# The end of an expert loop on Trainium2: one step moved, placement matrices built in pieces, one more tile summed by TensorE

## The chip, the core and the metric

The kernel runs on one core of one Trainium2 chip. The metric is the device time of a launch in microseconds; the median of three runs is used. A core has TensorE (PE, with its weight loads shown apart as PEld), VectorE (DVE), ScalarE (ACT), GpSimd (POOL) and SyncE (SP), which here issues most of the DMAs. Each engine works through its own queue in order and waits on semaphores.

## The reference

One transformer block over 512 rows of 1024: attention (left out here), a layer norm, a mixture of 32 experts in four groups of which each row uses two, and a second layer norm.

```python
SEQ, D_MODEL, N_GROUPS, EXPERTS_PER_GROUP, TOP_K, D_EXPERT = 512, 1024, 4, 8, 2, 256

def hierarchical_moe(x, w_group, b_group, w_expert, b_expert, w_gate, w_up, w_down):
    g_logits = (x @ w_group).astype(jnp.float32) + b_group
    g_prob = jax.nn.softmax(g_logits, axis=-1)
    g_gate, g_idx = lax.top_k(g_prob, 1)
    ...
    e_gate, e_idx = lax.top_k(e_prob, TOP_K)
    e_gate = e_gate / jnp.sum(e_gate, axis=-1, keepdims=True)
    combine = jnp.sum(jax.nn.one_hot(e_idx, EXPERTS_PER_GROUP, dtype=jnp.float32)
                      * e_gate[..., None], axis=2) * g_gate
    group_mask = jax.nn.one_hot(g_idx[..., 0], N_GROUPS, dtype=jnp.float32)
    y = jnp.zeros_like(x)
    for g in range(N_GROUPS):
        cw = (combine * group_mask[..., g:g + 1]).astype(x.dtype)
        hid = jax.nn.silu(jnp.einsum('bsd,edf->bsef', x, w_gate[g])) * jnp.einsum('bsd,edf->bsef', x, w_up[g])
        y = y + jnp.einsum('bsef,efd->bsd', hid * cw[..., None], w_down[g])
    return y

def reference(x, ...):
    for l in range(DEPTH):                                   # DEPTH is 1
        mix = hybrid_mixer(x, w_in[l], w_out[l], rel_bias[l])
        x = layer_norm(DEEPNORM_ALPHA * x + mix, ln1_g[l], ln1_b[l])
        ffn = hierarchical_moe(x, w_group[l], b_group[l], w_expert[l], b_expert[l],
                               w_gate[l], w_up[l], w_down[l])
        x = layer_norm(DEEPNORM_ALPHA * x + ffn, ln2_g[l], ln2_b[l])
    return x
```

## The kernel before

The 512 rows are T = 4 tiles of 128 (`hx`). After attention and the first layer norm, every row has a first and a second choice among the E = 32 experts; each expert has SLOTS = 64 places for rows. The part that the change touches is the loop over the experts and the stage behind it.

**The expert loop.** Experts go in pairs m; `get(m)` on GpSimd gathers a pair's rows into `xe`, TensorE turns them (`turn_x`). For an expert e TensorE does `gate_up(e)` (16 steps of 64 x 256 with `gate_w` and `up_w`), `turn_hidden(e)` (two transposes of the hidden rows) and `down(e)` (four products with `down_w`). Between them ScalarE does `silu(e)` and VectorE `product(e)` (the hidden rows) and `turned_out(e)` (the copy to `hidT`). Both engines copy one half each of down's result to `y_rows` (`first_half_out`, `second_half_out`), and GpSimd's `put(e)` scatters these to the DRAM table `expert_rows`, which has a row for each of the first and each of the second choices. Experts 30 and 31, the LAST pair, are not put: TensorE brings their rows to their places later. The order is written out by hand on each engine; TensorE's is: `gate_up(e+1)`, `turn_x` on odd e, the four transposes of `place` at e = 28 (L1590, behind a wait on all PLACED = 8 steps that build the matrices), `down(e)`, `turn_hidden(e+1)`.

**The weights.** Three matrices of 1 MB for each expert come over SyncE's queue into a ring of RING = 7 slots. `gate_w` and `up_w` of e are issued when `gate_up(e-7)` is done, `down_w` of e-1 behind them when its down is done. So the last ones are issued in the order gate/up 30, down 29, gate/up 31, down 30, down 31.

**The placement matrices.** `last_places` (L1133 to L1152) builds on VectorE: `again` (which row has which slot), then for both experts of the last pair `last_gate`, `gated` and `place`, and then diagonal matrices: `gate_diag` for the gates of each tile's second choices, `first_diag` for the first choices of tile BY_PE = 2. It stands behind expert 28's `turned_out` and uses the memory of ring slot 4, behind a wait on down 25.

**The last stage.** SyncE loads `first_y` and `second_y`, 512 KB for each tile, behind `put(28)` and `put(29)`. For each tile t TensorE adds in PSUM the rows of the last pair (`last_rows`, `place_T` by `y_rows`), for tile 2 the first-choice rows (`first_diag` by `first_y`) and the second-choice rows (`gate_diag` by `second_y`). VectorE does for the other tiles `add_first(t)` (L1230: `hx` plus gate by `first_y`), then for all `add_rest(t)` (L1239: plus the sum in PSUM, with the row sums for the mean; L1244: times `gain2`), and `finished(t)` (L1251) behind ScalarE's squares and root. SyncE stores each finished tile.

## Time and profile before

| | us |
|---|---|
| median of 3 runs (lowest, highest) | 566.36 (565.53, 567.29) |
| the profiled execution | 564.78 |
| its span | 563.1 |
| TensorE busy | 494.3 (88%) |
| VectorE busy | 250.3 (44%) |
| ScalarE busy | 184.1 (33%) |

The span is the time from the first to the last instruction of the profiled execution. The page puts 36% of the chain of work that ended last on TensorE, 9% on DMAs and 6% on VectorE. The share of busy time is an average over stages: in the expert loop the DMA engines are at 9 tenths or more of busy time in nearly every slice, in the last stage they are not. The rows further down are from the last 110 us.

### The profile page before, as it was taken

The page shows a single profiled execution, that of the slowest core. Times are in us where ns is not written, and L with a number is a line of the kernel's source. Part 1 is how long each engine was busy: PE and PEld are TensorE (multiplying, and loading weights), DVE is VectorE, ACT ScalarE, POOL GpSimd, SP SyncE. Part 2 cuts the span into 40 slices and gives each one's busy share as a digit, 9 for nine tenths or more (in the row PEclk, how much of TensorE's full clock was granted, in tenths as well). Part 3 has the DMA queues.
Part 4 walks back from the last instruction along what each step waited for, and adds up shares of the span by engine and source line. Part 5 has one row for each costly group of instructions (what it writes and reads, how often), then busy time and mean ns, then how long its engine had stood idle before and what let it go on. Part 6 is the DMA issues. An engine that isn't in the chain of part 4 may idle for free.

```text
span 563.1 us, 8062 instructions
## 1 busy us (share of the span) xinstructions
PE 494.3 (88%) x3068; PEld 326.1 (58%) x3068; DVE 250.3 (44%) x472; ACT 184.1 (33%) x377; POOL 149.3 (27%) x129
## 2 busy tenths in 40 slices
PE   4999999999999999799843899999998887878891
PEld 4788766766676766588632555555554454444440
DVE  3300256876766565600765533332332222215267
ACT  4212254465454555321513222322222222212222
POOL 3444435455413133133001222222222111210100
PEclk9999999999999999999975999999999998989997
DMA  6523221861211225199498799999999999999673
GB/s 242 169 76 113 75 75 39 319 105 38 76 38 38 76 75 208 56 348 420 167 415 307 321 370 416 414 415 415 414 415 418 415 416 418 415 416 417 245 273 149
DMA packets 53239, 144.12 MB, mean 256 GB/s; under 512 B 11014, under 2 KB 27414, under 8 KB 45008
## 3 DMA queue, kind: packets, MB, share of 16 engines
q1 hardware_dynamic: 48160, 134.40, 61.7%
q0 software_dynamic: 5040, 9.18, 4.4%
q8 instruction: 26, 0.43, 0.3%
q14 instruction: 13, 0.11, 0.1%
HBM read 135.45 MB, written 16.27 MB: 269 GB/s over the span
## 4 chain that ended last, share of the span: by engine, by line
PE 36%; DMA 9%; DVE 6%; issue 4%; SPq 2%; ACT 0%; POOLq 0%
PE bank L1498 16%; PE bank L1525 8%; DMA gate_w<-in_w_gate 5%; PE bank L1485 3%; DMA xe<-h_rows,idx_all 2%; PE bank L1278 2%; PE bank L1279 2%; PE bank L1280 2%; DMA second_y<-expert_rows 1%; SPq L379 1%; PE bank L1511 1%; DMA expert_rows<-y_rows,idx_odd 1%; PE bank L1500 1%; DVE hx L1239 1%; DVE hx L943 1%
## 5 line engine op out<-in xcount | busy, mean ns | idle before, releaser
L1498 PE MATMUL bank<-gate_w,xeT 128*64 128x256 f32 x512 | 122.7, 395 | 20.6 <-issue 18.9
L1500 PE MATMUL bank<-up_w,xeT 128*64 128x256 f32 x512 | 123.0, 396 | 0.0
L1498 PEld LDWEIGHTS bank<-gate_w,xeT 128*64 128x64 f32 x512 | 70.2, 142 | 54.4 <-issue 24.9
L513 POOL TENSOR_TENSOR w_lo<-raw,w_hi 128x1024 fp32r<-128x1024 f32 x28 | 71.2, 2543 | 89.2 <-ACT w_hi L629 89.2
L1500 PEld LDWEIGHTS bank<-up_w,xeT 128*64 128x64 f32 x512 | 70.2, 142 | 0.0
L1096 DVE TENSOR_TENSOR silu_hid<-silu_hid,bank 64x256 f32<-64x256 f32 x32 | 13.5, 423 | 117.8 <-ACT silu_hid L767 117.8
L1525 PE MATMUL bank<-down_w,hidT 128*64 128x512 f32 x256 | 61.3, 599 | 0.9 <-issue 0.9
L767 ACT ACTIVATE silu_hid<-bank 64x256 f32<-64x256 f32 x32 | 12.1, 377 | 129.9 <-PE bank L1500 129.9
L1278 PE MATMUL bank<-xT_hi,w_hi 128*128 128x512 f32 x128 | 53.6, 419 | 0.8 <-ACT values L648 0.8
L1280 PE MATMUL bank<-xT_lo,w_hi 128*128 128x512 f32 x128 | 50.7, 396 | 0.0
L1279 PE MATMUL bank<-xT_hi,w_lo 128*128 128x512 f32 x128 | 50.6, 395 | 0.0
L629 ACT ACTIVATE w_hi<-raw 128x1024 fp32r<-128x1024 f32 x28 | 29.6, 1057 | 42.9 <-PE bank L1280 27.2
L552 POOL DMA_INDIRECT xe<-h_rows,idx_all x16 | 17.2, 1076 | 79.5 <-PE bank L1485 68.4
L854 DVE TENSOR_TENSOR_SCAN fail<-fail 128x512 f32<-128x512 f32 (+3 forms) x32 | 27.0, 884 | 24.1 <-POOL fail L523 23.8
L669 ACT ACTIVATE wT<-bank 128x512 f32<-128x512 f32 (+3 forms) x64 | 24.3, 430 | 31.2 <-PE bank L1339 31.0
L1278 PEld LDWEIGHTS bank<-xT_hi,w_hi 128*128 128x128 f32 x128 | 24.1, 188 | 18.0 <-issue 11.4
L562 POOL DMA_INDIRECT expert_rows<-y_rows,idx_all x15 | 14.0, 934 | 73.5 <-DVE y_rows L1112 73.5
L1112 DVE COPY y_rows<-bank 64x512 f32<-64x512 f32 x32 | 22.2, 694 | 24.7 <-PE bank L1525 24.1
L1525 PEld LDWEIGHTS bank<-down_w,hidT 128*64 128x64 f32 x256 | 17.4, 136 | 22.9 <-issue 19.2
L758 ACT ACTIVATE xeT<-bank,shift_T,gain_T 128x128 f32<-128x128 f32 x64 | 24.1, 458 | 17.6 <-PE bank L1485 17.6
L775 ACT ACTIVATE y_rows<-bank 64x512 f32<-64x512 f32 x32 | 18.9, 591 | 30.7 <-PE bank L1525 30.3
L690 ACT ACTIVATE Z<-Z,nnear 128x512 f32<-128x512 f32 (+3 forms) x32 | 17.7, 555 | 34.2 <-DVE nnear L876 34.2
(183 smaller groups left out, 813.0 us busy)
## 6 DMA issues: line engine op xcount, KB each, us to landing
gate_w<-in_w_gate SPq DMA_DIRECT2D x32, 1024.0 KB, 24.8
up_w<-in_w_up SPq DMA_DIRECT2D x32, 1024.0 KB, 24.9
down_w<-in_w_down SPq DMA_DIRECT2D x32, 1024.0 KB, 24.4
raw<-in_w_in SPq DMA_DIRECT2D x24, 512.0 KB, 3.8
expert_rows<-xe SPq DMA_DIRECT2D x1, 4096.0 KB, 15.0
raw<-in_w_out SPq DMA_DIRECT2D x8, 512.0 KB, 4.3
hx<-in_x SPq DMA_DIRECT2D x4, 512.0 KB, 4.9
h_rows<-hx SPq DMA_DIRECT2D x4, 512.0 KB, 13.7
```

Of the source, the lines that this page charges most:

```text
L513: nc.gpsimd.tensor_tensor(lo[:, :], raw[:, slot, :], hi[:, :].bitcast(F32), ALU.subtract).then_inc(s_lo, 1)
L629: nc.scalar.activation(hi[:, :], raw[:, slot, :], ACT.Copy).then_inc(s_hi, 1)
L669: ins = nc.scalar.activation(wT[:, u % 2, h, 0:W[b]], TR[h][:, 0:W[b]], ACT.Copy)
L758: ins = nc.scalar.activation(xeT[:, m % 2, c, :], XE[:, c, :], ACT.Identity, bias=shift_T[:, c:c + 1], scale=gain_T[:, c:c + 1])
L854: ins = nc.vector.tensor_tensor_scan(f, f, f, 1.0, ALU.mult, ALU.min)
L1112: nc.vector.tensor_copy(y_rows[half(h), D // 2:], DN[h][1]).then_inc(s_yd, 1)
L1278: nc.tensor.matmul(dst, a_hi, b_hi, start=start, stop=False)
L1279: nc.tensor.matmul(dst, a_lo, b_hi, start=False, stop=False)
L1280: return nc.tensor.matmul(dst, a_hi, b_lo, start=False, stop=stop)
L1498: nc.tensor.matmul(GATE[h], xeT[:, m % 2, c, half(h)], gate_w[r][:, c, :], start=(c == 0), stop=(c == KD - 1))
L1500: mm = nc.tensor.matmul(UP[h], xeT[:, m % 2, c, half(h)], up_w[r][:, c, :], start=(c == 0), stop=(c == KD - 1))
L1525: mm = nc.tensor.matmul(DN[q][j], hidT[:, q, b, :], down_w[r][:, b, j * 512:(j + 1) * 512], start=(b == 0), stop=(b == FB - 1))
```

## The change

On TensorE, ScalarE and VectorE the loop gets a case of its own for e = 29 (E - 3): down 29 stands first, and gate/up 30 and 31 follow behind it, then the turn of expert 30's hidden rows; at e = 30 no gate/up is left. `last_places` is split: `slot_ranks` and expert 30's part stand behind `turned_out(26)`, expert 31's part behind `turned_out(27)`, the diagonals where the whole had stood, behind `turned_out(28)`. The wait of the first piece is on gate/up 25 rather than on down 25. BY_PE is now the tiles 2 and 3, so `first_diag` has two matrices, and VectorE's `add_first` for tile 3 is gone. On VectorE `add_rest(0)` stands ahead of `add_first(1)`.

```diff
...
         assert top[0] <= nc.sbuf_usable_end, (top[0], nc.sbuf_usable_end)
+        BY_PE = (T - 2, T - 1)
         spare = arena + 4 * SLOT
         again = at("again", [P, 2 * T, SLOTS], F32, spare)
         gated = at("gated", [P, 2 * T, SLOTS], F32, spare + 2048)
         place = at("place", [P, T, 2, SLOTS], F32, spare + 4096)
         place_T = at("place_T", [P, T, P], F32, spare + 6144)
         gate_diag = at("gate_diag", [P, T, P], F32, spare + 8192)
-        first_diag = at("first_diag", [P, P], F32, spare + 11264)
+        first_diag = at("first_diag", [P, len(BY_PE), P], F32, spare + 11264)
         last_gate = at("last_gate", [P, 2, 2, T], F32, spare + 10240)
         first_y = at("first_y", [P, T, D], F32, spare + SLOT)
         second_y = at("second_y", [P, T, D], F32, spare + SLOT + T * D * 4)
...
         PLACED = 8
         EARLY_AT = [(PAIRS - 2, 1), (PAIRS - 2, 3), (PAIRS - 1, 0), (PAIRS - 1, 1)]
-        BY_PE = T - 2
         def half(h):
...
             turned_half(1)
             first_half_out(0)
             for e in range(1, E):
-                if e + 1 < E:
+                if e == E - 3:
+                    first_half_out(e)
+                    silu(e + 1)
+                    silu(e + 2)
+                    continue
+                if e + 1 < E and e != E - 2:
                     silu(e + 1)
                 if e == E - 1:
                     nc.scalar.preload_act_table_set("sqrt_and_others")
...
                 ins.then_inc(s_place, 1)
                 dve.wait_ge(s_place, placed[0])
-            def last_places():
-                dve.wait_ge(s_dn, E - 6)
+            def slot_ranks():
+                dve.wait_ge(s_gu, E - 6)
                 then_place(nc.vector.tensor_tensor(
                     again[:, :, :], iota_f[:, :].unsqueeze(1).broadcast_to([P, 2 * T, SLOTS]),
                     rank[:, :, :].rearrange("p k t -> p (k t)").unsqueeze(2).broadcast_to([P, 2 * T, SLOTS]),
                     ALU.is_equal))
-                for h in range(2):
-                    then_place(nc.vector.tensor_tensor(last_gate[:, h, :, :], chosen[:, :, :, 2 * LAST + h],
-                                                       gate[:, :, :], ALU.mult))
-                    then_place(nc.vector.tensor_tensor(
-                        gated[:, :, :], again[:, :, :],
-                        last_gate[:, h, :, :].rearrange("p k t -> p (k t)").unsqueeze(2
-                                                                          ).broadcast_to([P, 2 * T, SLOTS]),
-                        ALU.mult))
-                    then_place(nc.vector.tensor_tensor(place[:, :, h, :], gated[:, 0:T, :], gated[:, T:, :], ALU.add))
+            def last_places(h):
+                then_place(nc.vector.tensor_tensor(last_gate[:, h, :, :], chosen[:, :, :, 2 * LAST + h],
+                                                   gate[:, :, :], ALU.mult))
+                then_place(nc.vector.tensor_tensor(
+                    gated[:, :, :], again[:, :, :],
+                    last_gate[:, h, :, :].rearrange("p k t -> p (k t)").unsqueeze(2).broadcast_to([P, 2 * T, SLOTS]),
+                    ALU.mult))
+                then_place(nc.vector.tensor_tensor(place[:, :, h, :], gated[:, 0:T, :], gated[:, T:, :], ALU.add))
+            def gate_diagonals():
                 for t in range(T):
                     ins = nc.vector.tensor_scalar(gate_diag[:, t, :], ident[:, :], gate[:, 1, t:t + 1], None, ALU.mult)
-                ins = nc.vector.tensor_scalar(first_diag[:, :], ident[:, :], gate[:, 0, BY_PE:BY_PE + 1], None, ALU.mult)
+                for j, t in enumerate(BY_PE):
+                    ins = nc.vector.tensor_scalar(first_diag[:, j, :], ident[:, :], gate[:, 0, t:t + 1], None, ALU.mult)
                 then_place(ins)
             n_passes = dve.value_load(passes_i[0:1, 0:1], min_val=1, max_val=S // SLOTS)
...
             turned_out(1)
             scaled_rows(3)
             for e in range(1, E):
-                if e + 1 < E:
+                if e == E - 3:
+                    second_half_out(e)
+                    product(e + 1)
+                    turned_out(e + 1)
+                    product(e + 2)
+                    continue
+                if e + 1 < E and e != E - 2:
                     product(e + 1)
                 if e % 2 == 1 and (e + 3) // 2 < MOE_PAIRS:
                     turned_tokens((e + 3) // 2)
                 second_half_out(e)
                 if e + 1 < E:
                     turned_out(e + 1)
+                if e == E - 7:
+                    slot_ranks()
+                    last_places(0)
+                if e == E - 6:
+                    last_places(1)
                 if e == E - 5:
-                    last_places()
+                    gate_diagonals()
                 if e == E - 4:
                     dve.wait_ge(s_turned, 1)
                     nc.vector.tensor_copy(place_T[:, :, :].rearrange("p t n -> p (t n)"), bank[:, 6, :]
...
             def add_rest(t):
                 n = T + t
-                if t != BY_PE:
-                    dve.wait_ge(s_res1, t + 1 if t < BY_PE else t)
+                if t not in BY_PE:
+                    dve.wait_ge(s_res1, t + 1)
                 dve.wait_ge(s_last, t + 1)
                 b = 2 * (T - 1 - t)
                 nc.vector.scalar_tensor_tensor(out=hx[:, t, :], in0=bank[:, b:b + 2, :].rearrange("p b n -> p (b n)"),
...
                                                in1=shift2[:, :], op0=ALU.mult, op1=ALU.add).then_inc(s_h, 1)
             add_first(0)
+            add_rest(0)
             add_first(1)
-            add_rest(0)
             add_rest(1)
             finished(0)
-            add_first(T - 1)
             for t in range(2, T):
                 add_rest(t)
                 finished(t - 1)
...
             down(0)
             turn_hidden(1)
             for e in range(1, E):
-                if e + 1 < E:
+                if e == E - 3:
+                    down(e)
+                    gate_up(e + 1)
+                    gate_up(e + 2)
+                    turn_hidden(e + 1)
+                    continue
+                if e + 1 < E and e != E - 2:
                     gate_up(e + 1)
                 if e % 2 == 1 and (e + 3) // 2 < MOE_PAIRS:
                     turn_x((e + 3) // 2)
...
                 b = 2 * (T - 1 - t)
                 pe.wait_ge(s_first[t], 32)
-                if t == BY_PE:
+                if t in BY_PE:
                     for j in range(2):
-                        nc.tensor.matmul(bank[:, b + j, :], first_diag[:, :], first_y[:, t, j * 512:(j + 1) * 512],
+                        nc.tensor.matmul(bank[:, b + j, :], first_diag[:, BY_PE.index(t), :], first_y[:, t, j * 512:(j + 1) * 512],
                                          start=False, stop=False)
                 for j in range(2):
                     mm = nc.tensor.matmul(bank[:, b + j, :], gate_diag[:, t, :], second_y[:, t, j * 512:(j + 1) * 512],
```

On TensorE, from the transposes of `place` to the end of the experts; `down_w0`, `1`, `2`, `3` are the ring slots of experts 28, 29, 30, 31, and `gate_w2`, `gate_w3` those of 30 and 31. Before:

```order
L1590 MATMUL bank<-ident_53,place_166 128x128 x4
L1525 MATMUL bank<-down_w0_106,hidT_163 64x512 x4
L1511 MATMUL bank<-ident_53,silu_hid_162 128x64 x2
L1498 MATMUL bank<-gate_w2_110,xeT_156 64x256
...
L1525 MATMUL bank<-down_w1_109,hidT_163 64x512 x4
L1511 MATMUL bank<-ident_53,silu_hid_162 128x64 x2
L1498 MATMUL bank<-gate_w3_113,xeT_156 64x256
...
L1525 MATMUL bank<-down_w2_112,hidT_163 64x512 x4
```

Now:

```order
L1616 MATMUL bank<-ident_53,place_166 128x128 x4
L1545 MATMUL bank<-down_w0_106,hidT_163 64x512 x4
L1531 MATMUL bank<-ident_53,silu_hid_162 128x64 x2
L1545 MATMUL bank<-down_w1_109,hidT_163 64x512 x4
L1518 MATMUL bank<-gate_w2_110,xeT_156 64x256
...
L1518 MATMUL bank<-gate_w3_113,xeT_156 64x256
...
L1531 MATMUL bank<-ident_53,silu_hid_162 128x64 x2
L1545 MATMUL bank<-down_w2_112,hidT_163 64x512 x4
```

Down 29 has moved ahead of gate/up 30, and the turn of expert 30's hidden rows from ahead of gate/up 31 to behind it.

On VectorE, the steps behind expert 28's `hidT`. Before:

```order
L1104 COPY hidT<-bank 128x128
L1136 TENSOR_TENSOR again<-iota_f,rank 128x512
L1141 TENSOR_TENSOR last_gate<-chosen,gate 128x8
L1143 TENSOR_TENSOR gated<-again,last_gate 128x512
L1148 TENSOR_TENSOR place<-gated 128x4x64
L1141 TENSOR_TENSOR last_gate<-chosen,gate 128x8
L1143 TENSOR_TENSOR gated<-again,last_gate 128x512
L1148 TENSOR_TENSOR place<-gated 128x4x64
L1150 TENSOR_SCALAR gate_diag<-ident,gate 128x128 x4
L1151 TENSOR_SCALAR first_diag<-ident,gate 128x128
L1096 TENSOR_TENSOR silu_hid<-silu_hid,bank 64x256
```

Now:

```order
L1109 COPY hidT<-bank 128x128
L1159 TENSOR_SCALAR gate_diag<-ident,gate 128x128 x4
L1161 TENSOR_SCALAR first_diag<-ident,gate 128x128 x2
L1101 TENSOR_TENSOR silu_hid<-silu_hid,bank 64x256
L1117 COPY y_rows<-bank 64x512
```

Seven steps have moved up to experts 26 and 27, and one diagonal is new.

On VectorE, the start of the last stage. Before:

```order
L1230 SCALAR_TENSOR_TENSOR hx<-first_y,gate,hx 128x1024 x2
L1239 SCALAR_TENSOR_TENSOR hx,row_sum<-bank,hx 128x1024
L916 TENSOR_SCALAR nmean<-row_sum 128x1
L1244 SCALAR_TENSOR_TENSOR first_y<-hx,nmean,gain2 128x1024
L1239 SCALAR_TENSOR_TENSOR hx,row_sum<-bank,hx 128x1024
L916 TENSOR_SCALAR nmean<-row_sum 128x1
L1244 SCALAR_TENSOR_TENSOR first_y<-hx,nmean,gain2 128x1024
L921 RECIPROCAL rstd<-std 128x1
L1251 SCALAR_TENSOR_TENSOR hx<-first_y,rstd,shift2 128x1024
L1230 SCALAR_TENSOR_TENSOR hx<-first_y,gate,hx 128x1024
```

Now:

```order
L1251 SCALAR_TENSOR_TENSOR hx<-first_y,gate,hx 128x1024
L1260 SCALAR_TENSOR_TENSOR hx,row_sum<-bank,hx 128x1024
L921 TENSOR_SCALAR nmean<-row_sum 128x1
L1265 SCALAR_TENSOR_TENSOR first_y<-hx,nmean,gain2 128x1024
L1251 SCALAR_TENSOR_TENSOR hx<-first_y,gate,hx 128x1024
L1260 SCALAR_TENSOR_TENSOR hx,row_sum<-bank,hx 128x1024
L921 TENSOR_SCALAR nmean<-row_sum 128x1
L1265 SCALAR_TENSOR_TENSOR first_y<-hx,nmean,gain2 128x1024
```

Tile 0 is taken whole ahead of tile 1's first-choice sum, and the third such sum (tile 3) is gone.

## Rows read from the trace of the kernel before

**Rows 1.** The chain that ended last: start us, us, what.

```profile
527.24 5.50 DMA expert_rows<-y_rows,idx_odd
...
534.12 7.07 DMA second_y<-expert_rows
541.21 1.30 DVE hx L1230
```

**Rows 2.** Timeline of VectorE: start us, us, engine, line, operation, count.

```profile
516.43 0.87 DVE L1150 TENSOR_SCALAR gate_diag<-ident,gate 128x128 f32<-128x128 f32 x4
517.21 0.28 DVE L1151 TENSOR_SCALAR first_diag<-ident,gate 128x128 f32<-128x128 f32 x1
```

**Rows 3.** Timeline of TensorE, experts 28 to 31; idle time before it in brackets.

```profile
517.55 0.66 PE L1590 MATMUL bank<-ident,place 128*128 128x128 f32 x4 [1.73 <-DVE first_diag L1151]
...
520.01 0.34 PE L1511 MATMUL bank<-ident,silu_hid 64*128 64x64 f32 x2
...
523.77 1.89 PE L1525 MATMUL bank<-down_w,hidT 128*64 128x512 f32 x8
...
526.54 0.40 PE L1498 MATMUL bank<-gate_w,xeT 128*64 128x256 f32 x1 [0.62 <-issue]
...
530.02 1.91 PE L1525 MATMUL bank<-down_w,hidT 128*64 128x512 f32 x8
...
533.09 1.94 PE L1525 MATMUL bank<-down_w,hidT 128*64 128x512 f32 x8 [0.89 <-issue]
535.90 1.96 PE L1605 MATMUL bank<-y_rows,place_T 128*128 128x512 f32 x4 [0.88 <-DVE y_rows L1112]
```

**Rows 4.** SyncE's queue, weights of 29 and 31; then issues, us to landing.

```profile
496.31 2.80 SPq L382 DMA_DIRECT2D down_w<-in_w_down  x1
499.16 1.06 SPq L376 DMA_DIRECT2D gate_w<-in_w_gate  x1
500.25 6.01 SPq L379 DMA_DIRECT2D up_w<-in_w_up  x1
...
gate_w<-in_w_gate SPq DMA_DIRECT2D x1, 1024.0 KB, 24.7
...
up_w<-in_w_up SPq DMA_DIRECT2D x1, 1024.0 KB, 26.2
```

**Rows 5.** Timeline of the last stage, VectorE and TensorE.

```profile
532.70 0.29 DVE L1104 COPY hidT<-bank 128x128 f32<-128x128 f32 x1
...
542.52 1.23 DVE L1239 SCALAR_TENSOR_TENSOR hx<-bank,hx 128x1024 f32<-128x1024 f32 x1
...
548.20 1.88 PE L1605 MATMUL bank<-y_rows,place_T 128*128 128x512 f32 x4
...
549.23 1.28 DVE L1230 SCALAR_TENSOR_TENSOR hx<-first_y,gate,hx 128x1024 f32<-128x1024 f32 x1
...
549.91 1.88 PE L1617 MATMUL bank<-second_y,gate_diag 128*128 128x512 f32 x4
...
550.42 1.22 DVE L1239 SCALAR_TENSOR_TENSOR hx<-bank,hx 128x1024 f32<-128x1024 f32 x1
...
554.47 1.22 DVE L1239 SCALAR_TENSOR_TENSOR hx<-bank,hx 128x1024 f32<-128x1024 f32 x1
```

**Rows 6.** TensorE's long pauses in the loop; two stretches, the granted clock third from the end.

```profile
452.03 0.40 PE L1498 MATMUL bank<-gate_w,xeT 128*64 128x256 f32 x1 [3.12 <-issue]
...
469.41 0.40 PE L1498 MATMUL bank<-gate_w,xeT 128*64 128x256 f32 x1 [3.74 <-issue]
...
485.88 0.40 PE L1498 MATMUL bank<-gate_w,xeT 128*64 128x256 f32 x1 [2.31 <-issue]
...
502.61 0.66 PE L1498 MATMUL bank<-gate_w,xeT 128*64 128x256 f32 x1 [3.12 <-issue]
...
472.00:473.00 1.00, 1.00 (x7) 0.64 (x5) 0.00 (x0) 0.00 (x0) 0.00 (x0) 0.50 1.08 438
...
504.00:508.00 4.00, 4.00 (x22) 2.59 (x20) 0.00 (x0) 0.00 (x0) 0.00 (x0) 0.50 1.03 422
```

## The prediction

> **What bounds the kernel now.** I read the chain of waits backwards first. Its end is one block on VectorE, from the sum of tile 1's first-choice rows at 541.21 us to the last output row, with only waits on its own pipeline in between; ahead of it stand the load `second_y` and, before that, the write of expert 29's rows into `expert_rows`, issued at 527.24 and landed 5.50 us later [rows 1]. The profiled execution took 564.78 us, which is 1.6 us below the median 566.36.
>
> Then TensorE's timeline over the last three experts [rows 3]. The reader is to see three things. Ahead of the four transposes of `place` it stands still for 1.73 us, released by `first_diag`. Gate/up of expert 31 starts at 526.54 after a pause of its own. And the queue says why: `up_w` of expert 31 was issued at 500.25 and landed 26.2 us later, at 526.45 [rows 4]. So the weight stream, not TensorE, sets when expert 31 starts, and nothing that saves time on TensorE ahead of 526.5 moves it. From there the kernel runs: gate/up 31 (3.48 us to 530.02), down 30, down 31 at 533.09, `y_rows`, and the first product of the last stage at 535.90 [rows 3]. I call this last moment S. All times here are of the kernel before unless I say "now".
>
> **1. Placement matrices in three pieces.** The same eight waited steps, one more diagonal. In the kernel before all stand behind expert 28's `hidT`, and TensorE waits. Now seven steps stand behind experts 26 and 27, where VectorE has its next work only after a whole gate/up (3.5 us). Only the diagonals stay: four took 0.87 us, the first-choice one 0.28 [rows 2], now two, so about 1.4 us from 513.0, over by 514.4, ahead of the end of gate/up 29 at 517.55 - 1.73 = 515.82. The stall of 1.73 us goes. What is late next: the hidden rows of 29, then down 29, which step 2 puts there.
>
> **2. Down 29 ahead of gate/up 30.** Turning the hidden rows of 29 moves from 520.01 to 518.3. Down 28 starts 0.6 us after the transposes do, now at 516.4, and one down can follow another after 3.07 us, as 31 follows 30 (533.09 less 530.02 [rows 3]). So down 29 could go at 519.5, if `down_w` of 29 were there. No row gives its landing. It was issued at 496.31, between expert 30's and 31's gate/up, and `gate_w` of 31 landed at 499.16 + 24.7 = 523.86 and `up_w` of 31 at 526.45, 2.59 us apart for 1 MB [rows 4]. One such step ahead of 523.86 gives 521.27; the 24.7 us of `gate_w` from its own issue give 521.0. I take 521.3. The bounds are 519.5 (not waited for) and 523.86. The Trainium skill, page "DMA: Bandwidth & Descriptors" (HWDGE ordering), says that completion is not first in, first out for each issuing engine, but that a semaphore increment lands only after every earlier write of the same DMA engine. By that rule the upper bound holds for transfers that use all 16 engines, and a landing later than that is no case here; no row shows it.
>
> So TensorE gets a **new wait** of about 2.7 us (518.6 to 521.3), and behind it in its queue stand gate/up 30 and 31. Down takes about 1.9 us (530.02, 1.91 [rows 3]), gate/up 3.48: 521.3 + 1.9 + 3.48 = 526.7, against 526.54 for `up_w` of 31. Expert 31 starts 0.15 us later than before. For bounds: landing at 519.5 costs nothing, landing at 523.86 gives 529.2, +2.7 us.
>
> The other half of this edit is on the path. Before, turning the hidden rows of 30 was done ahead of gate/up 31, and down 30 could start at once behind it at 530.02. Now gate/up 31 comes first, then the turn (0.34 us at 520.01), the copy of `hidT` on VectorE (0.29 us [rows 5]) and some 0.15 us for the hand-overs: **+0.78 us** for down 30, and from there to S everything keeps its distance (533.09 and 535.90, less 530.02). S now = 535.90 + 0.15 + 0.78 = 536.8.
>
> What it gives: down 29 starts 2.5 us earlier than 523.77. The write of its rows is issued at 524.8 and, with the same 5.50 us, lands at 530.3; SyncE then issues all eight loads of `first_y`/`second_y` that much earlier, and tile 1's second-choice rows are there at 538.7 instead of 541.2. ScalarE follows the same order; its silus of 30 and 31 are not waited for, since VectorE's product for 31 fits into the 1.9 us of down 30.
>
> **3. The last stage.** VectorE loses the sum for tile 3 (549.23 to the next start at 550.42, 1.19 us) and takes tile 0 whole ahead of tile 1's sum (1.31 us, 541.21 to 542.52). Its work from the start X of tile 0's rest to that of tile 3's was 554.47 - 542.52 = 11.95 us [rows 1, 5]; now 11.95 - 1.19 + 1.31 = 12.07. X no longer waits for tile 1's rows but for TensorE's second group: S + 1.82 + 1.88 = 540.5. By VectorE alone tile 3's rest would start at 552.6, 1.9 us earlier.
>
> But TensorE takes what VectorE gives. A group of two products with 512 columns costs 549.91 - 548.20 = 1.71 us, and the last ends 1.88 us after it starts [rows 5]. Before there were nine groups, S to 551.79, and tile 3's rest was 2.7 us behind them. Now there are ten and no transfer to wait for: 536.8 + 0.1 + 9 x 1.715 + 1.88 = **554.2**. That is after VectorE's 552.6, so TensorE decides, and tile 3's rest starts at 554.2 + 0.05 against 554.47. What follows (tile 3's own 4.2 us of steps and the last store) doesn't change.
>
> The page "TensorE: Matmul & The Clock Gate" of the Trainium skill (Back-to-back issue gap) gives N/2.4 + 2.5 ns, 216 ns for 512 columns, an isolated matmul at the high clock. Priced so, the added group is 0.43 us instead of 1.71 and TensorE ends at 552.9, for -1.5 us. The rows have four passes for each of these fp32 products, so I go by them.
>
> **Sum.** -0.2 us: start of 31 +0.15, down 30 +0.78, a tenth group +1.71 (2.5 in all, rounding aside) against the 2.7 us by which TensorE was ahead of VectorE at tile 3. Two pieces that each look like gains (1.73 us of stall, 1.9 us of VectorE) come to nothing, the first because the weights are not there, the second because the other engine ends later. 564.78 - 0.2 = 564.6 for such an execution; on the median, 566.1.
>
> **Rivals.**
> *A, the forecast:* 566.1, with 565.3 to 567.0 for the landing between 519.5 and some tenths after 521.3, and for noise.
> *B, the clock falls in the new wait (slower).* The trace has pauses of TensorE in the expert loop of 3.12, 3.74, 2.31 and 3.12 us. Around the 3.74 one and the last 3.12 one the granted clock went from 2.4 to 1.2 GHz (0.50 in the stretches from 472 and from 504), around the other two not: the first matmul after the last pause took 0.66 us, after the others 0.40 [rows 6]. The new pause has 2.7 us, just between, and unlike those it lies where nothing behind it has slack: gate/up 30 and 31 follow back to back. 4 us at half the clock cost 2.0 us; I take 1.2 to 2.7. The sum is then +1.0 to +2.5, 567.4 to 568.9. It decides from a pause of somewhere between 2.3 and 3.1 us, that is if `down_w` of 29 lands later than about 521.
> *C, VectorE decides.* If S stays nearly where it was (the turn and copy hidden, or the weights earlier) or TensorE's groups run closer, tile 3's rest starts between 552.6 and 553.3: -1.2 to -1.9 us, 564.5 to 565.2.
> *D, `down_w` of 29 lands at its upper bound:* +2.4 us, 568.8, with no change of clock.
> *E, the edit doesn't bring the loads forward*, as the write of 29's rows takes longer amid the weight stream. Tile 1's rows would come at 541 at the latest, as before; tile 1 isn't needed before about 543.2, so this stays in A.
>
> **How the numbers follow.** A 0.50 (with E), B 0.30, C 0.13, D 0.04, others 0.03. The predicted time is A's, 566.1. Two in ten may be left out: the range goes from 564.6 (most of C) to 568.5 (most of B). A difference of 0.3% (1.7 us) is about what a measurement can tell. Below 564.66 lies a third of C and little else, with some chance for scatter: 0.10. Above 568.06 lie some 60% of B, D and a little scatter: 0.27. The rest, 0.63, is same.
>
> **What the profile after would show.** Step 1: no pause ahead of the transposes of `place`. Step 2: a pause of 2 to 3 us ahead of down 29, started by `down_w` at 521.0 to 521.5; gate/up 31 at 526.5 to 526.8; the turn for 30 behind it; S at 536.7 to 537.0. Step 3: in the last stage TensorE without a pause, and VectorE waiting for it ahead of tiles 2 and 3. If VectorE isn't waiting there, C holds. If the granted clock is 0.5 in part of 520 to 530, B does. If down 29 starts at 519.5, its landing was sized wrongly, with no effect on S.

## The result and the profile after

| | before | changed |
|---|---|---|
| median us (lowest, highest), 19 runs each | 565.68 (563.87, 567.37) | 567.86 (565.64, 570.71) |
| the profiled execution | 564.78 | 565.64 |
| its span | 563.1 | 563.9 |

The ratio is 1.0037, 95% interval 1.0022 to 1.0051: the change costs about 2.1 us. The forecast was no difference, so it was wrong. The profiled execution is the fastest of the 19 of the changed kernel, so its time alone shows no loss; its last stretch, measured below from a fixed point, does.

TensorE's timeline of the changed kernel over experts 28 to 31 and the first and last group of the last stage (start us, us; in brackets the idle time before):

```profile
513.20 0.66 PE L1616 MATMUL bank<-ident,place 128*128 128x128 f32 x4
...
515.66 0.33 PE L1531 MATMUL bank<-ident,silu_hid 64*128 64x64 f32 x2
520.22 3.68 PE L1545 MATMUL bank<-down_w,hidT 128*64 128x512 f32 x8 [4.23 <-DMA down_w<-in_w_down]
...
531.97 1.94 PE L1545 MATMUL bank<-down_w,hidT 128*64 128x512 f32 x8 [0.43 <-issue]
...
535.06 1.94 PE L1545 MATMUL bank<-down_w,hidT 128*64 128x512 f32 x8 [0.89 <-issue]
...
537.88 1.96 PE L1631 MATMUL bank<-y_rows,place_T 128*128 128x512 f32 x4 [0.88 <-DVE y_rows L1117]
...
553.40 1.88 PE L1643 MATMUL bank<-second_y,gate_diag 128*128 128x512 f32 x4
```

Against [rows 3] the reader is to see: the pause ahead of the `place` transposes is gone; down 29 waits 4.23 us for its weights and then takes 3.68 us, where the same eight records (two for each of the four products) took 1.89; S, the first product of the last stage, is at 537.88.

The stretches of the same core (granted clock, DMA share and GB/s are the last three columns):

```profile
504.00:508.00 4.00, 3.77 (x24) 1.75 (x20) 2.23 (x6) 2.33 (x6) 0.00 (x0) 1.00 1.01 415
518.00:519.00 1.00, 0.00 (x0) 0.00 (x0) 0.00 (x0) 0.00 (x0) 0.20 (x1) 0.50 0.99 410
521.00:524.00 3.00, 3.00 (x10) 0.95 (x8) 0.05 (x1) 0.05 (x1) 0.00 (x0) 0.50 0.96 386
...
525.00:528.00 3.00, 3.00 (x32) 1.95 (x28) 0.00 (x0) 0.12 (x1) 0.90 (x1) 1.00 0.78 305
```

The granted clock fell from 2.4 to 1.2 GHz in the pause and came back in gate/up 30, at about 524.7. In the profile of the kernel before, this stretch is at the high level throughout, and the low stretch of that profile that comes last is at 504 to 508 [rows 6], where the profile after is at 1.00. The Trainium skill, page "TensorE: Matmul & The Clock Gate" (Part 1), says that the clock gate has these two levels only and that activity releases the lower one. The rows agree on the levels: 0.50 and 1.00 here, and mixed values elsewhere only in stretches that hold a change.

SyncE's queue, the issue of `up_w` of 31 with its us to landing, the chain that ended last, and VectorE's last steps, all of the changed kernel:

```profile
494.54 2.61 SPq L382 DMA_DIRECT2D down_w<-in_w_down  x1
...
498.65 6.48 SPq L379 DMA_DIRECT2D up_w<-in_w_up  x1
```

```profile
up_w<-in_w_up SPq DMA_DIRECT2D x1, 1024.0 KB, 26.8
```

```profile
494.54 25.64 DMA down_w<-in_w_down
520.22 3.68 PE bank L1545 x8
...
553.57 1.73 PE bank L1643 x4
555.32 1.24 DVE hx L1260 x2
```

```profile
541.66 1.22 DVE L1260 SCALAR_TENSOR_TENSOR hx<-bank,hx 128x1024 f32<-128x1024 f32 x1 [2.61 <-PE bank L1643]
...
550.17 1.23 DVE L1260 SCALAR_TENSOR_TENSOR hx<-bank,hx 128x1024 f32<-128x1024 f32 x1 [0.41 <-PE bank L1643]
...
555.32 1.23 DVE L1260 SCALAR_TENSOR_TENSOR hx<-bank,hx 128x1024 f32<-128x1024 f32 x1 [1.01 <-PE bank L1643]
...
559.57 1.28 DVE L1272 SCALAR_TENSOR_TENSOR hx<-first_y,rstd,shift 128x1024 f32<-128x1024 f32 x1
```

The chain now goes through the weights of expert 29 and TensorE, where it went through the loads of `second_y` and VectorE [rows 1]. `down_w` of 29 landed at 494.54 + 25.64 = 520.18 and `up_w` of 31 at 498.65 + 26.8 = 525.45. Against [rows 5], VectorE waits for TensorE at tiles 0, 2 and 3. Gate/up 31 started at 527.66, 2.2 us behind the landing of its last weights: TensorE, not the stream, now sets the start of expert 31.

**A measure that takes out the scatter.** The weight stream ends at another time in every execution: over the profiles of this study `up_w` of 31 landed (where TensorE waited for it, that is the start of gate/up 31 less 0.09) between 525.4 and 529.3 us, a wider scatter than any effect looked for. So I count from there. **L** is the time from the landing of `up_w` of 31 to the start of the last output row on VectorE, and **Z** the part of L behind S. Before: L = 558.70 - 526.45 = 32.3 and Z = 558.70 - 535.90 = 22.8. Changed: L = 559.57 - 525.45 = 34.1 and Z = 21.7. The difference in L, +1.9 us, is close to that of the medians (+2.1), though each L is one execution.

### The profile page after: what moved, and what is told of

Its sections match the earlier page's. It is cut to its first block, busy times and chain, and to the rows that moved or that the text cites. A ratio compares the mean times of both kernels' runs of the same rounds, so it can differ in the third digit from the quotient of the medians.

```text
span 563.9 us, 8069 instructions
## 1 busy us (share of the span) xinstructions
PE 498.8 (88%) x3072; PEld 326.8 (58%) x3072; DVE 249.4 (44%) x472; ACT 184.2 (33%) x377; POOL 149.4 (26%) x129
## 4 chain that ended last, share of the span: by engine, by line
PE 34%; DMA 17%; DVE 4%; issue 2%; SPq 1%; ACT 0%; POOLq 0%
PE bank L1518 14%; DMA gate_w<-in_w_gate 10%; PE bank L1545 6%; DMA down_w<-in_w_down 5%; DMA xe<-h_rows,idx_all 2%; PE bank L1505 2%; PE bank L1298 2%; PE bank L1300 2%; PE bank L1299 2%; PE bank L1631 1%; PE bank L1643 1%; PE bank L1531 1%; DVE hx L948 1%; PE bank L1451 1%; PE bank L1640 1%
## 5 line engine op out<-in xcount | busy, mean ns | idle before, releaser
L1518 PE MATMUL bank<-gate_w,xeT 128*64 128x256 f32 x512 | 124.3, 399 | 16.9 <-issue 15.2
L1520 PE MATMUL bank<-up_w,xeT 128*64 128x256 f32 x512 | 124.5, 400 | 0.0
L1545 PE MATMUL bank<-down_w,hidT 128*64 128x512 f32 x256 | 63.1, 614 | 5.5 <-DMA down_w<-in_w_down 4.2
L690 ACT ACTIVATE Z<-Z,nnear 128x512 f32<-128x512 f32 (+3 forms) x32 | 17.8, 556 | 34.1 <-DVE nnear L881 34.1
```

The source lines that it names most:

```text
L1518: nc.tensor.matmul(GATE[h], xeT[:, m % 2, c, half(h)], gate_w[r][:, c, :], start=(c == 0), stop=(c == KD - 1))
L1520: mm = nc.tensor.matmul(UP[h], xeT[:, m % 2, c, half(h)], up_w[r][:, c, :], start=(c == 0), stop=(c == KD - 1))
L1545: mm = nc.tensor.matmul(DN[q][j], hidT[:, q, b, :], down_w[r][:, b, j * 512:(j + 1) * 512], start=(b == 0), stop=(b == FB - 1))
```

## Experiments

Each expectation names theories by a letter. Theory W: down 29 now waits for its weights, the clock falls in that pause, and nothing behind it has slack. Theory G: the tenth group of products on TensorE loses. Theory T: the turn and the copy for expert 30, now behind gate/up 31, lose. For the last four runs, theory P: the last stage has two lengths, and which one it has depends on the loads.

### The order of experts alone, and the change without it

`e1_order_only` is the kernel before with this on TensorE, and the same order on ScalarE and VectorE:

```diff
             for e in range(1, E):
-                if e + 1 < E:
+                if e == E - 3:
+                    down(e)
+                    gate_up(e + 1)
+                    gate_up(e + 2)
+                    turn_hidden(e + 1)
+                    continue
+                if e + 1 < E and e != E - 2:
                     gate_up(e + 1)
```

> The kernel before with the new order of experts 29 to 31 alone; placement matrices and last stage as before. Theory W (the wait of down 29 for its weights, and the clock that falls in it, make the change slower): here the stall of 1.73 us ahead of the place transposes stays and splits the pause in two, so the wait for down_w is near 1 us and the clock falls in fewer executions. The last stage has nine groups, so VectorE starts tile 3's rest up to 2 us earlier than before: 0 to -2 us, ratio 0.9965 to 1.000, and the granted clock stays at 1.0 between 515 and 526. Theory G (the tenth group on TensorE alone makes it slower): no tenth group here, so also faster, -1 to -2 us. Theory T (the turn and copy for 30 behind gate/up 31, 0.78 us, and what follows on it): +0.8 us or more, ratio 1.0015 to 1.004.

Measured: 565.91 us, ratio 1.0006 (0.9985 to 1.0027). TensorE and a stretch of it:

```profile
521.80 3.68 PE L1536 MATMUL bank<-down_w,hidT 128*64 128x512 f32 x8 [4.25 <-DMA down_w<-in_w_down]
...
540.26 1.96 PE L1622 MATMUL bank<-y_rows,place_T 128*128 128x512 f32 x4 [0.88 <-DVE y_rows L1117]
```

```profile
522.00:527.00 5.00, 5.00 (x18) 1.77 (x18) 0.69 (x1) 0.59 (x1) 0.00 (x0) 0.50 0.85 343
```

The pause and the low clock are there as in the whole change, which the expectation denied: it counted on the stall for the placement matrices to split the pause, and here there is no such stall although the matrices are built in one piece. Gate/up 28 ran at the high clock, gate/up 29 then waited 1.81 us for weights, and VectorE was through in time. The stall in [rows 3] belongs to executions in which gate/up 28 ran slow, as in [rows 6]: with the old placement the profiles show it in all three of the kernel before and in `e5_two_tiles`, 1.52 to 1.74 us, each with the clock low in gate/up 28 or part of it, and not here. The median, on the other hand, doesn't show the 1.7 us that this profile's L of about 34.0 has against 32.3; the interval reaches to +1.5 us. It lies outside what each of the three theories expected (W and G faster, T slower), and the interval touches all three.

`e2_no_order` takes the new order out of the changed kernel and keeps the rest.

```diff
-                if e == E - 3:
-                    down(e)
-                    gate_up(e + 1)
-                    gate_up(e + 2)
-                    turn_hidden(e + 1)
-                    continue
-                if e + 1 < E and e != E - 2:
+                if e + 1 < E:
                     gate_up(e + 1)
```

> The changed kernel with the order of experts 29 to 31 as it was before; pieces and the two tiles summed by TensorE stay. Theory W: no new wait on down_w, start of the last stage (S) where it was, ten groups from there end at 553.3 against tile 3's rest at 554.47 before: -1.1 us, ratio 0.998. Theory G: +1.7 us, ratio 1.003, as with the whole change. Theory T: as W.

Measured: 565.36 us, ratio 1.0006 (0.9984 to 1.0028), with L = 31.1 and Z = 21.7. Without the new order the loss of 1.0037 is gone, which speaks against G as the whole of it; the interval still reaches to 1.0028. That the 1.2 us of gain in the profile is not in the median was open at this point.

### The pause filled

`e3_fill` is the changed kernel with three products that nobody reads in the pause. Nothing is left out.

```diff
                 if e == E - 3:
+                    pe.wait_ge(s_xeTs, MOE_PAIRS)
+                    pe.wait_ge(s_xeTa, MOE_PAIRS)
+                    for _ in range(3):
+                        nc.tensor.matmul(bank[:, 7, :], ident[:, :], xeT[:, LAST % 2, 0:4, :].rearrange("p c s -> p (c s)"),
+                                         start=True, stop=True)
                     down(e)
```

> The changed kernel with three extra 128 x 512 products into a PSUM bank that nobody reads (some 2.6 us at the high clock) between the turn of expert 29's hidden rows and down 29; they fill most of the pause of 4.23 us and change no result. Theory W: the granted clock stays at 1.0 from 515 to 526, down 29 takes 1.9 us instead of 3.7, gate/up 30 3.5 us, and the kernel is 1.5 to 2.5 us faster than the changed one: ratio to the kernel before 0.999 to 1.001. Theories G and T, without the clock: no gain, ratio 1.003 to 1.005.

Measured: 566.39 us, ratio 1.0013 (0.9994 to 1.0033); by the medians 1.5 us less than the changed kernel, though the two intervals overlap. TensorE's rows, the chain at the end of the wait, and two stretches:

```profile
518.94 0.33 PE L1531 MATMUL bank<-ident,silu_hid 64*128 64x64 f32 x2
519.20 2.84 PE L1606 MATMUL bank<-xeT,ident 128*128 128x512 f32 x6
```

```profile
497.82 25.64 DMA down_w<-in_w_down
523.51 1.94 PE bank L1545 x8
```

```profile
519.00:523.00 4.00, 3.04 (x9) 1.19 (x8) 1.58 (x3) 0.59 (x1) 0.90 (x1) 1.00 1.00 411
523.00:527.00 4.00, 3.49 (x24) 1.79 (x26) 0.69 (x1) 0.59 (x1) 0.00 (x0) 1.00 0.95 382
```

The weights come exactly as late, 25.64 us from their issue, and TensorE still waits for them; only it isn't idle. The clock stays at 1.00 and down 29 takes 1.94 us instead of 3.68. From down 29's start to S are 539.11 - 523.51 = 15.6 us against 537.88 - 520.22 = 17.7: 2.1 us are the clock's alone, in these two executions. L is 560.80 - 528.74 = 32.1.

### One tile by TensorE

`e4_one_tile` is the changed kernel with `BY_PE = (T - 2,)` and VectorE's sum for tile 3 back in its place behind `finished(0)`.

```diff
-        BY_PE = (T - 2, T - 1)
+        BY_PE = (T - 2,)
...
             finished(0)
+            add_first(T - 1)
             for t in range(2, T):
```

> The changed kernel with only tile 2 summed by TensorE (nine groups), tile 3's first-choice rows by VectorE as before; order of experts and pieces stay. Theory W: the wait and the low clock stay, S at 537.9; TensorE's nine groups end 1.7 us earlier and VectorE has 1.2 us more, so tile 3's rest moves by -0.7 us at most: ratio 1.002 to 1.004. Theory G: the tenth group is all of the loss: ratio 1.000 or below.

Measured: 566.99 us, ratio 1.0043 (1.0020 to 1.0066). Taking the tenth group out doesn't take the loss out, so G is not the whole of it.

```profile
520.11 0.34 PE L1532 MATMUL bank<-ident,silu_hid 64*128 64x64 f32 x2
523.09 2.95 PE L1546 MATMUL bank<-down_w,hidT 128*64 128x512 f32 x8 [2.65 <-DMA down_w<-in_w_down]
...
540.24 1.95 PE L1632 MATMUL bank<-y_rows,place_T 128*128 128x512 f32 x4 [0.88 <-DVE y_rows L1117]
```

In this execution gate/up 28 had run at the low clock, as in the first profile, and the wait was 2.65 us, which is the 2.7 us of the prediction's sum. The clock fell all the same, at about 523.9, behind the end of the wait and in down 29. From down 29's start to S are 17.15 us, 1.6 more than in `e3_fill`. Z is 561.51 - 540.24 = 21.3.

### Parts alone, and the load moved instead of the pause

`e5_two_tiles` is the kernel before with step 3 alone: `BY_PE` has both tiles, `first_diag` two matrices (not shown below), and the last stage its new order.

```diff
...
             add_first(0)
-            add_first(1)
             add_rest(0)
+            add_first(1)
             add_rest(1)
             finished(0)
-            add_first(T - 1)
```

> The kernel before with the two tiles summed by TensorE and tile 0 taken whole first; order of experts and placement pieces as before. Theory W (the new wait of down 29 and the clock in it carry the loss): no new wait, the last stage is 1.1 us shorter counted from S, its first product: ratio 0.998. If the last stage is what loses: 1.002 or more.

Measured: 566.48 us, ratio 1.0025 (1.0003 to 1.0046): slower, where W had it faster. It is the other case of the expectation, that the last stage loses, and so the tenth group, by itself, is not free. TensorE ahead of expert 31 and at S, and a stretch behind the pause:

```profile
529.15 0.56 PE L1498 MATMUL bank<-gate_w,xeT 128*64 128x256 f32 x1 [2.34 <-issue]
...
540.20 1.95 PE L1605 MATMUL bank<-y_rows,place_T 128*128 128x512 f32 x4 [0.88 <-DVE y_rows L1112]
```

```profile
530.00:532.00 2.00, 2.00 (x12) 1.43 (x10) 0.00 (x0) 0.00 (x0) 0.00 (x0) 0.50 0.21 72
```

A pause of 2.34 us ahead of gate/up 31, in an order that hadn't been changed, and the clock fell right behind it, at about 529.3. So the kernel before may well have this fall in some executions too. Z is 561.88 - 540.20 = 21.7, as with every kernel with ten groups. What the kernel before makes of a late S is shown further down.

`e6_early_load` is the whole change with `down_w` of 29 issued ahead of expert 30's gate and up.

```diff
+                if e == E - 2:
+                    next_down(e - 1)
                 expert_matrix(e % RING, e, 0)
                 expert_matrix(e % RING, e, 1)
...
-                if e > RING:
+                if e > RING and e != E - 2:
                     next_down(e - 1)
```

> The whole change, and SyncE issues down_w of expert 29 ahead of gate_w and up_w of 30 instead of behind them; no byte more or less. Theory W: down 29 finds its weights there, TensorE's pause goes to ahead of gate/up 30 and is about 1 us, the granted clock stays at 1.0 from 516 to 527, and what is left of the loss is the 0.78 us of turn and copy against 1.1 us of the last stage: ratio 0.9985 to 1.0005. Theory T (the turn and the copy for 30, and what hangs on them, carry the loss, the wait for weights does not): ratio 1.003 to 1.004, as with the whole change.

Measured: 566.76 us, ratio 1.0020 (0.9995 to 1.0045), between the two expectations; the interval holds both no loss and the loss of the whole change, so the time doesn't decide. The trace is as W has it:

```profile
520.44 1.94 PE L1547 MATMUL bank<-down_w,hidT 128*64 128x512 f32 x8 [0.90 <-issue]
...
523.80 0.40 PE L1520 MATMUL bank<-gate_w,xeT 128*64 128x256 f32 x1 [1.43 <-issue]
...
529.41 0.40 PE L1520 MATMUL bank<-gate_w,xeT 128*64 128x256 f32 x1 [1.94 <-issue]
...
539.70 1.95 PE L1633 MATMUL bank<-y_rows,place_T 128*128 128x512 f32 x4 [0.88 <-DVE y_rows L1119]
```

```profile
516.00:527.00 11.00, 8.67 (x60) 4.61 (x58) 2.70 (x5) 1.55 (x3) 1.79 (x2) 1.00 0.99 405
```

One wait of 4.2 us has become three of 0.9 to 1.9, and the clock stays high in this execution. From gate/up 31 to S are 10.29 us, against 535.90 - 526.54 = 9.36 before: 0.93 us for the turn and the copy, theory T's term, at its own price. L = 32.1.

`e7_pieces_only` is the kernel before with step 1 alone: `slot_ranks`, `last_places(0)`, `last_places(1)` and `gate_diagonals` at the places of the change.

```diff
+                if e == E - 7:
+                    slot_ranks()
+                    last_places(0)
+                if e == E - 6:
+                    last_places(1)
                 if e == E - 5:
-                    last_places()
+                    gate_diagonals()
```

> The kernel before with the placement matrices in three pieces alone. Both theories: TensorE does not wait for the placement matrices, but gate/up 31 waits for up_w all the longer; no gain, ratio 0.999 to 1.001.

Measured: 564.30 us, ratio 0.9997 (0.9971 to 1.0024), with L = 32.2 and Z = 22.7: nothing gained, as both said. Its trace has one thing that bears on theory W:

```profile
518.22 0.40 PE L1508 MATMUL bank<-gate_w,xeT 128*64 128x256 f32 x1 [1.74 <-issue]
...
518.71 0.63 PE L1508 MATMUL bank<-gate_w,xeT 128*64 128x256 f32 x1
...
520.00:521.00 1.00, 1.00 (x8) 0.75 (x6) 0.00 (x0) 0.00 (x0) 0.00 (x0) 0.50 1.01 410
```

The clock fell at the start of gate/up 30, behind a pause of only 1.74 us. It cost nothing here, since gate/up 31 still had to wait 0.52 us for its weights.

`e8_turn_first` is `e6_early_load` with the turn of 30 between the two gate/ups.

```diff
                     gate_up(e + 1)
-                    gate_up(e + 2)
                     turn_hidden(e + 1)
+                    gate_up(e + 2)
```

> As e6_early_load, and TensorE turns expert 30's hidden rows between gate/up 30 and gate/up 31, where it waits for up_w of 31 in any case. Theory W: no long pause, down 30 starts at once behind gate/up 31, so S stands 9.4 us behind the start of gate/up 31 as before instead of 10.1; the last stage gives its 1.1 us: ratio 0.997 to 0.999, the fastest of all. Theory T: the same gain against the whole change, 0.8 us and more, but not below 1.001, since the loads are not what it names.

Measured: 564.48 us, ratio 0.9992 (0.9973 to 1.0012).

```profile
527.62 0.40 PE L1520 MATMUL bank<-gate_w,xeT 128*64 128x256 f32 x1 [0.68 <-issue]
...
536.98 1.96 PE L1633 MATMUL bank<-y_rows,place_T 128*128 128x512 f32 x4 [0.88 <-DVE y_rows L1119]
```

The turn fits into the wait for `up_w` of 31 and the 0.93 us are gone (536.98 - 527.62 = 9.36). L = 31.1. All of the change is in this kernel but the place of the turn for 30, and the 2.1 us are not. Which of the two edits gives how much, the medians don't tell: `e6_early_load` alone is not clearly faster than the changed kernel.

### The last stage and the kernel before once more

`e9_best_mix` is `e8_turn_first` with the last stage of the kernel before.

```diff
-        BY_PE = (T - 2, T - 1)
+        BY_PE = (T - 2,)
...
             add_first(0)
-            add_rest(0)
             add_first(1)
+            add_rest(0)
             add_rest(1)
             finished(0)
+            add_first(T - 1)
```

> As e8_turn_first, but the last stage as before: only tile 2's first-choice rows by TensorE, and both first sums ahead of tile 0's rest. Theory P (the length of the last stage depends on whether the rows of tile 1 are there when TensorE has tile 0's sum ready; where they are, nine groups take 20.75 us from S to the last output row, against 21.69 with ten): from S 20.7 to 20.9 us, and from the start of gate/up 31 some 30.1 us instead of 32.2 in the kernel before: ratio 0.996 to 0.998. Its rival, that two tiles by TensorE are always the shorter stage: 22 to 23 us from S, ratio 0.999 to 1.002, slower than e8_turn_first.

Measured: 564.45 us, ratio 0.9976 (0.9951 to 1.0001), the best of all, though its interval still touches 1. VectorE:

```profile
539.84 1.28 DVE L1253 SCALAR_TENSOR_TENSOR hx<-first_y,gate,hx 128x1024 f32<-128x1024 f32 x1 [1.16 <-DMA second_y<-expert_rows]
541.16 1.23 DVE L1262 SCALAR_TENSOR_TENSOR hx<-bank,hx 128x1024 f32<-128x1024 f32 x1
...
557.34 1.28 DVE L1274 SCALAR_TENSOR_TENSOR hx<-first_y,rstd,shift 128x1024 f32<-128x1024 f32 x1
```

Z = 557.34 - 536.59 = 20.75 with nine groups, 0.9 us shorter than with ten. L = 30.2.

`e10_tile3_early` is `e9_best_mix`, but loads tile 3 ahead of tile 2 and sums its first-choice rows ahead of tile 0's rest.

```diff
-            for t in range(T):
+            for t in (0, 1, 3, 2):
                 sp.dma_start(first_y[:, t, :], y_v[:, 0, t, :]).then_inc(s_first[t], 16)
...
             add_first(0)
             add_first(1)
+            add_first(T - 1)
             add_rest(0)
             add_rest(1)
             finished(0)
-            add_first(T - 1)
```

> As e9_best_mix, with tile 3's rows loaded ahead of tile 2's and its first sum, too, ahead of tile 0's rest, where VectorE waits for TensorE. Theory P: VectorE has 1.2 us less behind S + 3.9, TensorE's nine groups decide by 1 us: 19.9 to 20.3 us from S to the last output row, ratio 0.995 to 0.997. If the rows of tile 3 come later than S + 2.5, the sum holds up tile 0's rest and nothing is gained against e9_best_mix.

Measured: 565.74 us, ratio 1.0008 (0.9987 to 1.0030). The rows of tile 3 are there only at 542.5, 5.75 us behind S, so the sum holds up tile 0's rest until 543.82. Z = 558.80 - 536.75 = 22.05: the second half of the expectation.

`e11_before_again` and `e12_before_third` are the kernel before, for its trace.

> The kernel before once more, for a second look at its end. Theory P: where S comes more than 9.4 us behind the start of gate/up 31 (low clock in it) or the loads come early, the last stage takes 20.8 to 22 us, not 22.8; the first profile was one of the long ones.

> The kernel before a third time. Theory P as in e11_before_again: the distance from S to the last output row is between 20.7 and 22.8 us and is long where tile 1's rows come later than 4 us behind S.

One execution each, 565.05 and 564.25 us. The first one's gate/up 31, a stretch behind it, S, and its chain at the end:

```profile
527.15 0.40 PE L1498 MATMUL bank<-gate_w,xeT 128*64 128x256 f32 x1 [2.17 <-issue]
```

```profile
528.00:530.00 2.00, 2.00 (x13) 1.36 (x11) 0.00 (x0) 0.00 (x0) 0.00 (x0) 0.50 0.63 240
```

```profile
538.20 1.96 PE bank L1605 x4
540.15 1.72 PE bank L1617 x4
...
558.95 1.28 DVE hx L1251
```

The clock fell here too, 0.3 us behind the end of the pause, S came 11.05 us behind the start of gate/up 31 instead of 9.36, and yet L is 558.95 - 527.06 = 31.9, no more than without the fall. The last stage took it up: Z = 20.75. The loads of tile 1 hang on down 29, which is ahead of the fall, and were there at 540.6, 1.3 us ahead of TensorE's sum for tile 0, so they held up next to nothing. In the third execution the clock stayed high, S was early, tile 1's rows came 5.4 us behind it, and Z was 22.9, as in the first profile. **Where S is early, the kernel before has slack of some 2 us between S and the loads, and the change takes it away.**

| kernel | pause near the end, us | clock fell in it or within 0.8 us behind | L | Z | ratio |
|---|---|---|---|---|---|
| before, three profiles | 0.62; 2.17; 0.55 | no; yes; no | 32.3; 31.9; 32.3 | 22.8; 20.8; 22.9 | 1 |
| changed | 4.23 | yes | 34.1 | 21.7 | 1.0037 |
| e1_order_only | 4.25 | yes | about 34.0 | 20.8 | 1.0006 |
| e4_one_tile | 2.65 | yes | about 33.4 | 21.3 | 1.0043 |
| e3_fill | 1.47 | no | 32.1 | 21.7 | 1.0013 |
| e5_two_tiles | 2.34 | yes | 32.8 | 21.7 | 1.0025 |
| e6_early_load | 1.94 | no | 32.1 | 21.7 | 1.0020 |
| e2_no_order | 2.37 | no | 31.1 | 21.7 | 1.0006 |
| e7_pieces_only | 0.52 | no (but behind one of 1.74) | 32.2 | 22.7 | 0.9997 |
| e8_turn_first | 0.68 | no | 31.1 | 21.7 | 0.9992 |
| e10_tile3_early | 0.67 | no | 31.5 | 22.1 | 1.0008 |
| e9_best_mix | 0.68 | no | 30.2 | 20.8 | 0.9976 |

The pause is the one ahead of down 29 for the changed kernel, `e1_order_only`, `e4_one_tile` and `e3_fill`, and the one ahead of gate/up 31 for the others. For `e1_order_only` and `e4_one_tile` the landing of `up_w` of 31 isn't in the trace; for the first it is put 5.27 us behind that of `down_w` of 29, as in the changed kernel, for the second 2.6 us behind that of `gate_w` of 31, by the 2.59 of [rows 4]. L is one execution, the ratio an average over many, so they need not agree in every row; still, the lowest L and the lowest ratio are the same kernel's, and the two kernels with the highest ratios are among the three with the highest L.

## Why the prediction was wrong, point by point

**Step 1 was right in its place and wrong in what it stood on.** The pause ahead of `place` is gone (513.20, no bracket), and it gained nothing alone. But the stall of 1.73 us is no constant of the kernel: it was there in the profiles in which gate/up 28 had run at the low clock. `e1_order_only` shows the old placement without it.

**Step 2, the landing, was right.** `down_w` of 29 landed 5.27 us ahead of `up_w` of 31; the sum had 526.45 - 521.27 = 5.18.

**Step 2, the wait: this is the step that failed.** The prediction had "a new wait of about 2.7 us" and gave the clock's fall in it a chance of 0.30, as rival B, with +1.2 to +2.7 us. The wait began at the turn for 29 as it stood in one profile, moved up by the stall. That profile's gate/up 28 ran slow; where it doesn't, the turn is done 1.5 us earlier against the stream, at 515.99, and the wait is 4.2 us instead of 2.7 (4.23, 4.25, and 1.47 behind the products of `e3_fill`). Where gate/up 28 did run slow, in `e4_one_tile`, the wait was 2.65, so the sum was right for its own profile and wrong for others. The trace itself had it: a pause that ends with a transfer gets longer by all that the work ahead of it gets faster. With 4.2 us it is longer than any pause in [rows 6], and the fall should have been the forecast. In the terms of the sum, "start of 31 +0.15" became 2.2 us behind the landing instead of 0.24: 2.0 us more than forecast. B's price was right for this execution, 2.1 us by the changed kernel against `e3_fill`; by the same stretch it was 2.9 in `e1_order_only` and 1.6 in `e4_one_tile`. B's point of decision, a pause between 2.3 and 3.1 us, was wrong in kind: there is no such point. All three long waits of down 29 that weren't filled had a fall (4.25, 4.23, 2.65), but so had pauses of 2.34, 2.17 and 1.74 us, while pauses of 2.37 us near the end and of 3.12 [rows 6] to 3.14 us (`e6_early_load`, at 505.01) had none. So between 1.7 and 3.1 us the length alone doesn't decide; what else does is open.

**Step 2, turn and copy.** 0.78 us in the sum, 0.93 measured (`e6_early_load` against 9.36). The term is real in the trace and is taken away by the order in `e8_turn_first`.

**Step 3.** From S to tile 3's rest the sum had 554.25 - 536.8 = 17.45; measured 555.32 - 537.88 = 17.44, with VectorE waiting for TensorE at tiles 0, 2 and 3 as forecast. (The rows show two records for each product, not the "four passes" that the prediction reads in them; its price of 1.71 us for a group was measured and right.) But what it was set against was wrong. The sum took the 22.8 us of the kernel before as its last stage, and so counted 1.1 us as saved. Where S is late the same stage takes 20.75 (`e11_before_again`), and then ten groups cost 0.9 us, which fits `e5_two_tiles` being slower. So the forecast's -0.2 us holds only against an execution like the first profile, and with the clock high.

**Rivals.** B held, with 567.86 inside its 567.4 to 568.9. That the time lies inside the stated range is B's doing, to which the forecast gave 0.30; the account that the forecast went by did not hold. C (VectorE decides) did not: [1.01 <-PE] at tile 3. D did not: the landing was where the sum put it. E was put into A, rightly as to time: tile 1's rows were not waited for.

**What stays open.** Theory T's term and B's add up to 0.9 + 2.1, less the 1.1 of the last stage: 1.9, the loss by the two profiles, against 2.1 by the medians. How often the clock falls in either kernel isn't shown: there are 3 profiles of the one and one of the other, with two more that share its order. The split between clock, turn and last stage therefore rests on single profiles; what the medians carry is that the loss goes with the new order (`e2_no_order`) and that it goes when the load and the turn are moved too (`e8_turn_first`). And `e1_order_only`, with the low clock in its profile, isn't slower in the median than the kernel before; its interval allows +1.5 us, not quite the +1.7 of its L. The fall cost 2.9 us in that profile; at the 2.1 of the changed kernel's its L would be about 33.2, or +0.9 (an estimate from these figures), which the interval does allow.

## What to carry to other kernels

If a step is moved ahead of another to free what hangs on it, its own inputs must be moved first: here one line in the loads' order cut the wait of 4.2 us that the new order had made to 0.9, and it took a better place for the turn besides to get the time back. A pause on TensorE can cost more than its length if what follows has no slack, since the clock may fall in it or right behind it. And a term taken from one profile is to be asked what it would be in another execution: the stall, the pause and the length of the last stage all differed with where the clock had fallen before.

## What the runs showed of the hardware

- With 2.6 us of products that nobody reads in a pause of 4.2 us, the clock stayed at 2.4 GHz, and the eight records behind took 1.94 instead of 3.68 us. That is one profile; the three with the same wait unfilled all had the fall.
- The clock fell in or within 0.8 us behind pauses of 1.74, 2.17, 2.34 and 2.65 us, and not at one of 2.37, one of 3.12 [rows 6] and one of 3.14: within this stretch of lengths it differs from execution to execution.
- The same stream of weights ended between 525.4 and 529.3 us over the profiles, while `up_w` of 31 took 26 to 27 us from issue to landing in each that shows it. In the three profiles of the kernel before, the end of the stream differs by 1.2 us and L by 0.4, so it may well be most of the scatter of some 4 us between runs of one kernel; that, and what upstream moves it, isn't shown.
